# Two more tiles of the first gated network as seven-product pairs, their operand sums made earlier

## The reference, cut to what matters

```
h  = silu(x @ w_gate) * (x @ w_up)      # 512 x 2816, from 512 x 1024
y  = h @ w_down                         # 512 x 1024
x1 = layer_norm(ALPHA * x + 0.5 * y)    # after the first network
```

## Time and profile before

| | us |
|---|---|
| three timed runs | 1612.23, 1614.64, 1616.84 |
| their median | 1614.64 |
| the profiled execution, whole | 1613.68 |
| its span, from the first to the last instruction | 1611.8 |
| PE busy in the span | 1598.5 |
| DVE busy | 1037.2 |
| ACT busy | 794.8 |
| POOL busy | 528.0 |

### The profile page before, as it was taken

How to read it: one execution, slowest core, us unless ns; L and a number is a source line. 1 busy time by engine, 2 the same in 40 slices (tenths; PEclk the granted TensorE clock), 3 DMA queues, 4 the chain that set the end, 5 groups by cost and what they waited for, 6 DMA issues and landing times.

```text
span 1611.8 us, 25969 instructions
## 1 busy us (share of the span) xinstructions
PE 1598.5 (99%) x10319; PEld 1438.3 (89%) x10319; DVE 1037.2 (64%) x1470; ACT 794.8 (49%) x1355; POOL 528.0 (33%) x329
## 2 busy tenths in 40 slices
PE   9999999999999999999999999999999999999999
PEld 7989989998888888889899989998768988998998
DVE  5936749567565767556945848657863593674852
ACT  4534536457445455446543536557474353353641
POOL 3150322355563443133150231344333314022132
PEclk9999999999999999999999999999999999999999
DMA  7332333353221445222243343351113223333332
GB/s 204 104 105 86 105 99 107 106 148 85 66 75 57 129 123 154 66 79 79 79 118 92 93 118 105 106 157 46 42 38 79 79 84 113 91 101 110 106 105 79
DMA packets 296066, 157.92 MB, mean 98 GB/s; under 512 B 5265, under 2 KB 292618, under 8 KB 295946
## 3 DMA queue, kind: packets, MB, share of 16 engines
q1 hardware_dynamic: 295946, 156.26, 34.0%
HBM read 154.14 MB, written 2.10 MB: 97 GB/s over the span
## 4 chain that ended last, share of the span: by engine, by line
PE 89%; DVE 6%; ACT 2%; issue 1%; DMA 1%; POOL 0%; SPq 0%; DVEq 0%; POOLq 0%
PE bank L2739 11%; PE bank L2735 11%; PE bank L2736 11%; PE bank L611 9%; PE bank L612 9%; PE bank L615 9%; PE bank L2629 2%; PE bank L2625 2%; PE bank L2626 2%; PE bank L655 2%; PE bank L654 2%; PE bank L659 2%; PE bank L3207 2%; PE bank L634 1%; PE bank L635 1%
## 5 line engine op out<-in xcount | busy, mean ns | idle before, releaser
L519 POOL TENSOR_TENSOR wlo<-wraw,whi 128x1024 fp32r<-128x1024 f32 (+1 forms) x121 | 287.3, 2380 | 368.1 <-ACT whi L514 368.1
L514 ACT CAST whi<-wraw 128x1024 fp32r<-128x1024 f32 (+1 forms) x268 | 274.8, 1029 | 209.7 <-PE bank L615 82.0
L1723 POOL TENSOR_TENSOR hid<-hval,hid 128x512 fp32r<-128x512 f32 x54 | 98.6, 1826 | 527.4 <-ACT hid L1341 527.4
L519 DVE TENSOR_TENSOR wlo<-wraw,whi 128x1024 fp32r<-128x1024 f32 (+1 forms) x147 | 186.7, 1274 | 29.9 <-ACT whi L514 22.8
L1853 DVE SCALAR_TENSOR_TENSOR res<-res,bank 128x512 f32<-128x512 f32 x78 | 52.6, 684 | 215.4 <-PE bank L615 124.1
L611 PE MATMUL bank<-ahi,whi 128*128 128x512 f32 x430 | 171.7, 399 | 0.0
L612 PE MATMUL bank<-alo,whi 128*128 128x512 f32 x430 | 167.7, 390 | 0.0
L611 PE MATMUL bank<-hid,whi 128*128 128x512 f32 x316 | 123.2, 390 | 0.0
L612 PE MATMUL bank<-hid,whi 128*128 128x512 f32 x316 | 123.0, 389 | 0.0
L615 PE MATMUL bank<-ahi,wlo 128*128 128x512 f32 x430 | 107.6, 389 | 0.0
L2735 PE MATMUL bank<-ahi,whi 128*128 128x256 f32 x432 | 106.2, 280 | 0.0
(11 more groups left out here) (433 smaller groups left out, 4226.9 us busy)
## 6 DMA issues: line engine op xcount, KB each, us to landing
wraw<-in_ffn_w_gate SPq DMA_DIRECT2D x42, 512.0 KB, 3.9
wraw<-in_ffn_w_up SPq DMA_DIRECT2D x42, 512.0 KB, 4.6
wraw<-in_ffn_w_down SPq DMA_DIRECT2D x32, 512.0 KB, 4.7
wraw<-in_w_in SPq DMA_DIRECT2D x30, 512.0 KB, 3.8
wraw<-in_w_gate SPq DMA_DIRECT2D x21, 512.0 KB, 3.9
wraw<-in_w_up SPq DMA_DIRECT2D x21, 512.0 KB, 4.4
wraw<-in_w_out SPq DMA_DIRECT2D x16, 512.0 KB, 4.3
wraw<-in_w_down SPq DMA_DIRECT2D x16, 512.0 KB, 4.6
```

The source lines that it names most:

```text
L514: eng.copy(high_of(b)[:, 0:n], raw_of(b)[:, 0:n]).then_inc(hi_ready, 1)
L519: eng.tensor_tensor(low_of(b)[:, 0:n], raw_of(b)[:, 0:n], high_of(b)[:, 0:n], ALU.subtract).then_inc(LO[b][0], 1)
L1723: pool.tensor_tensor(hlo[:, p.m, :], hval[:, p.tile % 2, :], hhi[:, p.m, :], ALU.subtract).then_inc(hidden_ready, 1)
```

## The change

In f1 the pairs begin with tile 2 instead of tile 4, so 20 of 22 tiles are pairs. f2 and f3 stay as they are. In f1's first part DVE makes the four operand sums and their low halves right behind its last `keep_x` copy, ahead of the plain tiles; ACT makes their high halves at the matching place, right behind block 2's high half. The weight sums of the first pair move from the third plain tile's place to the first one's (the conditions `2 * first - 3` and `2 * first - 2`). Four weight blocks (4 to 7) lose their low halves on POOL and get them on DVE as part of pairs.

```diff
@@ -30,7 +30,7 @@
 LN_EPS = 1e-5
 RMS_EPS = 1e-6
 PARTS = (8, 6, 8)
-FIRST_FAST = (4, 0, 0)
+FIRST_FAST = {"f1": (2, 0, 0), "f2": (4, 0, 0), "f3": (4, 0, 0)}
 assert sum(PARTS) * P == F
 RAW = 6
 BANKS = 4
@@ -327,7 +327,7 @@
         for f in range(3):
             for part, tiles in enumerate(PARTS):
                 ph = phases[f"f{f + 1}_up{part}"]
-                for m in range(FIRST_FAST[part], tiles):
+                for m in range(FIRST_FAST[ph.name[:2]][part], tiles):
                     PAIRS[ph.name, m] = Pair(len(PAIRS), f, ph, m)
         PAIR_LIST = list(PAIRS.values())
         PAIR_BLOCKS = {b for p in PAIR_LIST for b in (p.gate, p.up)}
@@ -338,7 +338,7 @@
             return PAIRS.get((ph.name, m))
 
         def first_pair(ph):
-            return pair_of(ph, FIRST_FAST[int(ph.name[-1])])
+            return pair_of(ph, FIRST_FAST[ph.name[:2]][int(ph.name[-1])])
 
         raw_ready = [sem(f"raw_ready{i}") for i in range(RAW)]
         hi_ready = sem("hi_ready")
@@ -732,7 +732,7 @@
         HI_OF = {"out": 0, "xq": 8}
         SUM_STEPS = KD - 1
 
-        OPENING = {p.n for p in PAIR_LIST if p.m == FIRST_FAST[int(p.ph.name[-1])]}
+        OPENING = {p.n for p in PAIR_LIST if p.m == FIRST_FAST[p.ph.name[:2]][int(p.ph.name[-1])]}
 
         class Counts:
 
@@ -1375,8 +1375,10 @@
 
                 for part in range(len(PARTS)):
                     ph, down = phases[f"{name}_up{part}"], phases[f"{name}_down{part}"]
-                    t0, first = part_tile0(ph.name), FIRST_FAST[part]
-
+                    t0, first = part_tile0(ph.name), FIRST_FAST[name][part]
+
+                    if first == 2:
+                        turned_high(first_pair(ph), (T3, T1, T2, T4))
                     for j in range(2 * first):
                         if j == 2 * first - 2:
                             pair_hi(first_pair(ph))
@@ -1387,7 +1389,7 @@
                             split_hi(act, first_pair(ph).gate)
                         if j or ph.base == 0 or part:
                             hi_stream(ph, j)
-                        if j == 3:
+                        if j == 3 and first > 2:
                             turned_high(first_pair(ph), (T3, T1))
                         if j == 4:
                             turned_high(first_pair(ph), (T2, T4))
@@ -1725,7 +1727,7 @@
             def ffn(name, last):
                 for part in range(len(PARTS)):
                     ph, down = phases[f"{name}_up{part}"], phases[f"{name}_down{part}"]
-                    first = FIRST_FAST[part]
+                    first = FIRST_FAST[name][part]
                     for j in range(2 * first):
                         if j or ph.base == 0 or part:
                             lo_stream(ph, j)
@@ -2122,13 +2124,16 @@
             def ffn(name, alpha, scale, last, once=None):
                 for part in range(len(PARTS)):
                     ph = phases[f"{name}_up{part}"]
-                    t0, first = part_tile0(ph.name), FIRST_FAST[part]
+                    t0, first = part_tile0(ph.name), FIRST_FAST[name][part]
+                    if first == 2:
+                        turn_operand(first_pair(ph))
+                        turned_low(first_pair(ph), (T3, T1, T2, T4))
                     for j in range(2 * first):
                         if j % 2:
                             hidden(ph, j, t0, scale)
                         if j or ph.base == 0 or part:
                             lo_stream(ph, j)
-                        if j == 3:
+                        if j == 3 and first > 2:
                             turn_operand(first_pair(ph))
                             turned_low(first_pair(ph), (T3, T1))
                         if j == 4:
@@ -2810,7 +2815,7 @@
 
             def ffn(name, last, once=None):
                 for part in range(len(PARTS)):
-                    ph, first = phases[f"{name}_up{part}"], FIRST_FAST[part]
+                    ph, first = phases[f"{name}_up{part}"], FIRST_FAST[name][part]
                     if ph.base == 0:
                         first_blocks(ph)
                     for j in range(0 if part else 2 if ph.base == 0 else 4, 2 * first):
```

## The result

The changed kernel takes 1616.63 us (median of 18 runs, 1614.49 to 1619.20) against 1614.32 for the kernel before (18 runs, 1612.23 to 1616.84): the ratio is 1.0015, with a 95% interval of 1.0009 to 1.0021. It is slower, by 2.3 us: the interval leaves no doubt of the direction, but the amount is less than the 0.3% (4.8 us) that the prediction took as the least difference. The forecast, 1620.0, was 3.4 us too high; 0.4 of that is the base (a median of three, 1614.64, where eighteen give 1614.32) and rounding. The range held the time with 0.3 us to spare, which is luck rather than accuracy, and of the three outcomes the one given 0.40 came, not the one given 0.56.

What follows compares the result with a forecast made beforehand. PE's own work bounds the kernel, busy 1598.5 of 1611.8 us. Waits of 4.34 + 1.37 + 0.89 + 0.65 = 7.25, less 1.96 saved, give +5.3 on 1614.64: 1619.9, say 1620; range 1616.3 to 1623.3.

Steps and rivals of the forecast that it cites:

- the three outcomes: Whole kernel against before, beyond or within about 0.3% (4.8 us): slower 0.56, same 0.40, faster 0.04.
- The saving per pair, 0.98: PE in f1: a pair costs 9.90 against 10.88 for a plain tile; two tiles save 1.96 us.
- The chain over ACT and DVE to block 3, a wait of 4.34: Opening: ACT's operand casts wait for DVE's sums, so block 3 starts at 32.3, not 27.96; PE waits 4.34 us.
- POOL and DVE meet, sums at 36.15: Opening: POOL's block 3 low half holds up DVE's hidden tile 0 cast; first pair's weight sums start at 36.15.
- The second to fourth wait, 1.37, 0.89 and 0.65: PE waits for DVE's low halves: first pair's first product 1.37, its seventh 0.89, next pair's first product 0.65 us.
- the clock falls and is hidden: Block 3: one 1.2 GHz stretch after the first wait costs PE 1.5 us, covered by 2.26 of later waits; adds 0.
- The clock's rival, a fall at every gap: Opening's four waits: the clock falls more than once; +1.6 us on top, 1621.5; chance 0.20.
- The rival's other form, a low clock for longer: Opening: the clock stays low for two stretches; same rival, +1.6 us on top, 1621.5, chance 0.20.
- The fourth product ends at 51.95, two pairs more make 71.75: f1's first part: old trace reaches the same state at 66.46, so the opening is +5.3 us behind.
- From there each pair's sums wait only for the pair two before it, as in the old trace, and 9.90 a pair holds.: f1's pairs from 51.95 on: no further PE wait, each pair 9.90 us.
- My clock estimate: At the wait ending at 576.47: 15 matmuls at 0.209 instead of 0.109 us, so one slow stretch costs 1.5 us.
- The delay isn't given back: Behind the opening: nothing runs to a fixed time, so the +5.3 us stays to the end.

Runs made afterwards that it cites:

- turn4_early: Changed kernel's early operand sums alone, with four plain tiles in f1 as in the kernel before; 1619.99 us, ratio 1.0031 to before.
- hi3_first: Changed kernel with block 3's high half cast on ACT ahead of the operand sums' casts; 1618.72 us, ratio 1.0026 to before.
- wait_before: Kernel before, PE waiting in each part's first pair for ACT's copy of the first product; 1602.16 us, ratio 0.9922; again 1603.19, 0.9925.
- wait_after: Changed kernel, PE waiting for ACT's first-product copy in the first pair of every part except f1's first; 1606.38 us, ratio 0.9951 to before.
- a2_again: Changed kernel without any edit, run a third time for a trace alone; a single run of 1616.02 us.
- first3_lo_dve: Changed kernel with three plain tiles in f1, block 3's high half cast earlier, low halves of blocks 3 to 5 on DVE; 1611.94 us, ratio 0.9985 to before.

## Why the prediction was right or wrong

- **The saving per pair, 0.98.** Right at the slow pace (pairs of 9.90 in the profiled execution). At the fast pace it is 1.36.
- **The chain over ACT and DVE to block 3, a wait of 4.34.** Right: 4.25, 4.24 and 4.24 in three executions. turn4_early shows that the early sums alone make it.
- **POOL and DVE meet, sums at 36.15.** Right: 36.07. hi3_first shows the same meeting at another instruction of DVE (3.37 in place of 1.23). The Trainium skill, "SBUF — State Buffer", section "Who interferes with whom", says that DVE and GpSimd share a pair of ports under an exclusive lock; the rows agree (1.78 beside POOL, 0.43 without).
- **The second to fourth wait, 1.37, 0.89 and 0.65; the clock falls and is hidden.** The second and third are right together, and the fourth is 0.56. The fall lengthens block 3 by 1.58, and of these two waits 0.39 is left: 1.97 in place of 2.26. In the prediction's words, PE was "ahead of DVE's low halves, and those do not depend on PE".
- **The clock's rival, a fall at every gap.** Not borne out: the waits of 0.2 to 0.6 in the changed kernel lowered nothing, nor did nine of 0.45 in wait_before, whose mean clock is 1.00. What the prediction cited from the Trainium skill, "TensorE: Matmul & The Clock Gate", section "HAM oscillation — how this bites in real kernels", does not reach gaps this short here. The rival's other form, a low clock for longer, came once in four openings: in wait_after the clock was 0.50 up to 35.2 and 0.73 on average from there to 38.2, and block 3 took 7.86. It cost nothing, since the low half of the next pair's first product started 26.06 after block 2 in all four.
- **The fourth product ends at 51.95, two pairs more make 71.75.** Right in the profiled execution (51.49 + 0.47 = 51.96, and 71.28 + 0.47 = 71.75). Up to here, +5.3 stands to within 0.1.
- **"From there each pair's sums wait only for the pair two before it, as in the old trace, and 9.90 a pair holds."** This is the step that failed. The mechanism in it is right (no wait appears), but the size of a pair is not a constant of the program: it is 9.90 or 9.52. The old opening has no wait of PE and ran at 9.90; the new waits restart PE, and in three of the four traces of this opening (wait_after has it too) the pairs behind them took 9.52, which gives back 1.9 of the 5.3 within the part. The two openings measured so, +5.3 and +3.4, would make 1619.6 and 1617.7 from the median of before.

The trace of before held a sign of this. The pairs of f2's and f3's first part, which begin with a wait, ran at 113.6 ns a matmul, those elsewhere at 117.8. I had taken the pair's cost from one place of f1. My clock estimate held another sign: it has 0.109 us for a 256-column matmul at the full clock, beside pairs at 0.118. (The 0.109 itself is 2.40 divided by a count that takes in the matmuls at both ends; the starts there are 113.3 ns apart. The 1.5 us worked out from it stands.)

"The delay isn't given back" did not hold in full either. PE's wait at L634, which ends near 576 in before, is 2.46 to 2.68 in the four traces of kernels with four plain tiles in f1, and 1.90 to 1.95 in the eight with two or three. So some 0.6 comes back there; why is not known.

What stays open: the medians of the two measurements, +2.3 and +3.9, lie about the +3.4 of the fast opening, but the first is 1 us below it, of which the shorter wait at L634 would be some 0.6, and how often each pace came in the timed runs was not measured. There is spread from elsewhere too: a2_again is 1.3 us shorter behind `vrow` than before is, with a slower f2 in it, because its wait at L634 is shorter and the clock did not fall behind it. That the two groups among the 18 times are the two paces of f1's first part is an inference: a slow-paced execution was in the upper one, and no other of the 18 has a trace.

## What to carry to other kernels

Before a wait is priced, look at what the engine does behind it as well: the cost of the same work can depend on whether the engine was restarted. Measure the distance of the matmuls in every stage that has them, not in one, and where a program has two values of it, try to force the better. And a step moved ahead of what an engine waits for has to be costed along the whole chain: taking one link out (hi3_first) only moved the wait.

## What the runs showed of the hardware that was not expected

- Matmuls of 256 columns in fp32r, one behind the other, run at 113.3 or 117.8 ns from start to start, both at a granted clock of 1.00. The state holds over dozens of products. What the state is stays open: the weight loads alternate with the matmuls one to one in both. A load starts 3.3 ns after the matmul ahead of its own in both, and its own matmul follows the load's start by 110.0 ns at the fast pace (wait_before, 60 to 90) and by 114.4 at the slow one (before, 60 to 90), so the whole difference lies in that step. The Trainium skill, "TensorE: Matmul & The Clock Gate", section "Wait — 56ns, not 53.3ns?", gives columns at 2.4 GHz and about 2.5 ns more; for 256 columns that would be an estimate of 109 ns. Neither pace is that, and that section has one value where these products have two.
- A wait of 0.45 us, made on purpose at nine places, took 12.2 us off 1614.3.
- A late start of 0.12 us was enough once to bring the fast pace (first3_lo_dve), while a wait of 0.56 could end it (after, at 48.56: 113.4 ns ahead of it, 117.8 behind).
- A wait of PE of around 2 us lowers the clock in some executions and not in others: behind the 2.46 of the earlier trace rows it fell, behind one of 2.60 at the same work in wait_before it did not. At that place it fell in nine of the twelve traces, behind waits of 1.91 to 2.68, and not in a2_again (1.90), first3_lo_dve (1.95) and wait_before.
